# Attention of a hybrid backbone: one loop of iterations over all units, and softmax maps combined by two GpSimd passes without normalising

## The reference, cut to what matters

```
s  = einsum('bqhcd,bkhcd->bhcqk', q, k) * scale          # c = 0, 1: two maps
pr = softmax(s, axis=-1)
w  = pr[:, :, 0] - lam * pr[:, :, 1]
o  = einsum('bhqk,bkhe->bqhe', w, v)
o  = rms_norm(o, subln_g) * (1.0 - lam_init)              # mean of o*o + 1e-6 under the root
```

## Time and profile before

| | |
|---|---|
| time, median of 3 runs | 4578.49 us |
| span of the profiled execution | 4593.8 us |
| busy: PE, DVE, ACT, POOL | 3727.9, 1665.4, 1256.8, 1175.2 us |
| share of the span: PE, DVE, ACT, POOL | 81, 36, 27, 26% |
| attention, in either layer | 375 us of the span |
| busy in the first layer's attention: PE, DVE, ACT, POOL | 255.8, 231.9, 207.6, 140.8 us |

### The profile page before, as it was taken

The page is one execution under the profiler, slowest core; times in us unless marked ns, Lnnn a source line. Parts: engine busy times, 40 slices in busy tenths (PEclk is TensorE's granted clock), DMA queues, the critical chain, the costliest instruction groups (busy, mean ns, idle before and its releaser), DMA issues. The chain is left out here.

```text
span 4593.8 us, 53336 instructions
## 1 busy us (share of the span) xinstructions
PE 3727.9 (81%) x19468; PEld 3375.5 (73%) x19468; DVE 1665.4 (36%) x1950; ACT 1256.8 (27%) x1848; POOL 1175.2 (26%) x542
## 2 busy tenths in 40 slices
PE   3874999787577799999938849997875777999998
PEld 2664988565466699999926649885664567999998
DVE  4234323254666412121242343232546664121212
ACT  2232122122455412121122321221224563121211
POOL 2011121054343222212120121210543342212211
PEclk8877999888787899999968779998887888999999
DMA  2544211234511111110415442122445111111104
GB/s 85 185 132 182 87 64 71 93 128 160 173 36 45 46 54 65 34 68 30 141 54 185 135 180 87 63 78 88 134 157 167 37 44 53 51 62 37 64 32 149
DMA packets 156156, 428.99 MB, mean 93 GB/s; under 512 B 30202, under 2 KB 51966, under 8 KB 154688
## 3 DMA queue, kind: packets, MB, share of 16 engines
q1 hardware_dynamic: 139936, 379.55, 24.8%
q10 hardware_dynamic: 16128, 48.26, 2.9%
HBM read 312.38 MB, written 120.08 MB: 94 GB/s over the span
## 5 line engine op out<-in xcount | busy, mean ns | idle before, releaser
L2061 POOL TENSOR_TENSOR branch_wl<-branch_raw,branch_wh 128x1536 fp32r<-128x1536 f32 (+1 forms) x72 | 267.3, 3713 | 926.5 <-ACT branch_wh L2021 926.5
L127 PE MATMUL ps<-hh,branch_wh 128*128 128x384 f32 x1728 | 398.2, 338 | 41.2 <-POOL branch_wl L2061 24.2
L127 PE MATMUL ps<-hl,branch_wh 128*128 128x384 f32 x1728 | 396.2, 337 | 0.0
L127 PE MATMUL ps<-hh,branch_wl 128*128 128x384 f32 x1728 | 396.1, 337 | 0.0
L127 PEld LDWEIGHTS ps<-hh,branch_wh 128*128 128x128 f32 x1728 | 311.5, 190 | 44.5 <-issue 44.5
L2092 DVE TENSOR_TENSOR branch_gate<-ps,branch_gate 128x1152 f32<-128x1152 f32 x48 | 65.2, 1358 | 751.8 <-PE ps L127 751.8
L127 PEld LDWEIGHTS ps<-hl,branch_wh 128*128 128x128 f32 x1728 | 311.9, 190 | 0.0
L127 PEld LDWEIGHTS ps<-hh,branch_wl 128*128 128x128 f32 x1728 | 311.5, 190 | 0.0
L1292 POOL TENSOR_TENSOR conv_dl<-conv_draw,conv_dh 128x512 fp32r<-128x512 f32 x128 | 180.2, 1415 | 471.4 <-ACT conv_dh L1242 470.6
L1778 POOL TENSOR_TENSOR attn_prob<-attn_prob 128x1280 f32<-128x1280 f32 (+1 forms) x72 | 190.4, 2644 | 241.1 <-ACT attn_prob L1690 241.1
L127 PE MATMUL ps<-hh,mixin_wh 128*128 128x384 f32 x720 | 167.2, 340 | 102.2 <-POOL mixin_wl L943 97.0
(11 more groups left out here) (262 smaller groups left out, 8421.2 us busy)
## 6 DMA issues: line engine op xcount, KB each, us to landing
branch_raw<-in_w_mo SPq DMA_DIRECT2D x48, 768.0 KB, 4.2
H_dram<-fspec_hout ACTq DMA_DIRECT2D x100, 256.0 KB
fspec_araw<-in_w_ada SPq DMA_DIRECT2D x48, 512.0 KB, 4.6
conv_hs<-H_dram SPq DMA_DIRECT2D x32, 768.0 KB, 4.5
w_in_raw<-in_w_in SPq DMA_DIRECT2D x44, 512.0 KB, 3.8
fspec_draw<-in_dft_taps SPq DMA_DIRECT2D x68, 256.0 KB, 3.0
conv_draw<-in_dft_fwd SPq DMA_DIRECT2D x64, 256.0 KB, 2.6
conv_draw<-in_dft_inv SPq DMA_DIRECT2D x64, 256.0 KB, 2.6
```

What stands on the lines that cost most here:

```text
L127: last = pe.matmul(out, w[:, k, :], x[:, k, cols], start=(k == 0 and n == 0), stop=(k == kt - 1 and n == 2))
L2061: pool.tensor_tensor(wl[:, b, 0:size], raw[:, b, 0:size], wh[:, b, 0:size].bitcast(F32), ALU.subtract).then_inc(S["lo"], 1)
```

## The change

Every engine's body of a head becomes `for i in range(NU)`. In iteration i the same four things are in flight everywhere: scores of unit i+1, softmax of unit i, fill 0 of the transposes of unit i-1, fills 1 and 2 of unit i-2, and the group products and norms some iterations later (`units_of`, `group_at`). Where i-1 or i-2 is below zero, the unit belongs to the head before, so the tail of a head runs inside the first iterations of the next, on all engines. Behind the last head come 5 iterations (`DRAIN`) without new units. The body is written out for head 0, as a loop for heads 1 and 2, for head 3 and for the drain.

The combination changes: instead of `prob0/s0 - lam*prob1/s1`, the weights are `prob0 + ratio*prob1` with `ratio = -lam*s0/s1`. The factor s0 is left in the weights, cancels in the norm, and the constant becomes `EPS*s0*s0` per query (`es`). The DVE pass over `prob0` and the ACT pass over `prob1` are gone; POOL multiplies `prob1` and then adds.

Between heads, ACT also rounds the queries (was DVE). Map 0's key remainder moves from POOL to DVE. The prompt unit's weights have their own buffers `wph` and `wpl`, and the prompt values are split one iteration after the others. SP stores the last groups of a head around the next head's loads.

```
 # DVE, per unit
-chain(dve.reciprocal(rinv[:], total[:, u % 2]))
-chain(dve.tensor_tensor(rinv[:, 1:2], rinv[:, 1:2], lam[:, 3:4], ALU.mult))
-dve.sem_inc(S["rp"], 1)
-dve.tensor_scalar(prob0[:, u % 3, 0:n], prob0[:, u % 3, 0:n], rinv[:, 0:1], None, ALU.mult)
+s0, s1 = total[:, u % 3, 0:1], total[:, u % 3, 1:2]
+dve.reciprocal(rinv[:], s1).then_inc(S["rc"], 1)
+dve.scalar_tensor_tensor(out=es[:, u:u + 1], in0=s0, scalar=EPS, in1=s0, op0=ALU.mult, op1=ALU.mult)
+dve.wait_ge(S["rc"], NU * h + u + 1)
+dve.scalar_tensor_tensor(out=ratio[:, u % 3:u % 3 + 1], in0=s0, scalar=lam[:, 3:4], in1=rinv[:],
+                         op0=ALU.mult, op1=ALU.mult).then_inc(S["rp"], 1)
 # ACT, per unit
-nc.scalar.activation(prob1[:, u % 2, 0:n], prob1[:, u % 2, 0:n], ACT.Copy, scale=rinv[:, 1:2])
 # POOL, per unit
+pool.tensor_tensor(gone[:], ratio[:, u % 3:u % 3 + 1], ratio[:, u % 3:u % 3 + 1], ALU.add)
+pool.tensor_scalar(prob1[:, u % 2, 0:n], prob1[:, u % 2, 0:n], ratio[:, u % 3:u % 3 + 1], None, ALU.mult
+                   ).then_inc(S["sc"], 1)
+pool.wait_ge(S["sc"], NU * h + u + 1)
 pool.tensor_tensor(prob0[:, u % 3, 0:n], prob0[:, u % 3, 0:n], prob1[:, u % 2, 0:n], ALU.add)
 # PE, the order of an iteration
+turn(h, two, 1)
+with_v(h, group_at(i, 4, prev, cur), 0)
+done = group_at(i, 5, prev, cur)
+with_v(h, done, 1)
+turn(h, two, 2)
+scores(h, i + 1, 0)                 # at i = 8: scores(h + 1, 0, 0)
+sums(h, done)
+turn(h, one, 0)
+spread(h, done)
+scores(h, i + 1, 1)                 # at i = 8: scores(h + 1, 0, 1)
+if i == NU - 2 and more: turn_keys(h + 1)
 # ACT, the order of an iteration
+high(h, two, 1, prev)
+softmax(h, i, 0, prev)
+high(h, two, 2, prev)
+take(h, group_at(i, 5, prev, cur))
+softmax(h, i, 1, prev)
+high(h, one, 0, prev)
+if i == 2 and cur: split_values(h, prev)
+if i == 3 and cur: split_prompt_values(h, prev)
+if i == NU - 2 and more: split_keys(h + 1, False); split_rest(h + 1, False)
 # POOL, the order of an iteration
+inverse_root(h, group_at(i, 5, prev, cur))
+combine(h, i)
+if i == 2 and cur: lower_values(h)          # waits for both value splits of ACT
+if i == NU - 2 and more: lower_keys(h + 1)  # map 1 only
 # DVE, the order of an iteration
+maximum(h, i, 0)
+low(h, two, 1)
+maximum(h, i, 1)
+low(h, two, 2)
+if i == NU - 1 and more: split_lower(h + 1, False)
+means(h, done)
+ratios(h, i)
+low(h, one, 0)
+scale(h, done)
 # ACT, between heads
+for c in range(2):
+    nc.scalar.copy(kh[:, c, 0:TS], kraw[:, c, 0:TS]).then_inc(S["kh"], 1)
+nc.scalar.copy(qs[:], qraw[:]).then_inc(S["qh"], 1)
 # DVE, between heads (split_lower), ahead of what split_queries had
+dve.tensor_tensor(kl[:, 0, 0:TS], kraw[:, 0, 0:TS], kh[:, 0, 0:TS].bitcast(F32), ALU.subtract)
-dve.tensor_copy(qs[:], qraw[:]).then_inc(S["qh"], 1)
```

More of the change, by code:

```diff
@@ L1459, in group, with weights, units_of, at @@
             return (TS, P) if g == NPV - 1 else (g * G * P, G * P)
[L1461 to L1473, removed]
+        def weights(big, small, u, at, cnt):
+            if u == QT:
+                return small[:, at:at + cnt, :]
+            q = (u % G) * P
+            return big[:, (u // G) % 2, at:at + cnt, q:q + P]
+        def units_of(i, prev, cur):
+            def at(j):
+                if j < 0:
+                    return (-1, j + NU) if prev else None
+                return (0, j) if cur and j < NU else None
+            return at(i), at(i - 1), at(i - 2)
+        def group_at(i, shift, prev, cur):
+            for d, have in ((-1, prev), (0, cur)):
+                for g in range(NPV):
+                    step = 2 * g + shift if g < NPV - 1 else NU + 3
+                    if have and i - d * NU == step:
+                        return d, g
+            return None
         with nc.Block() as block:
@@ L1495, in load_values, with store @@
                     sp.dma_start(vraw[:, KT], vrows[QT, :, hc]).then_inc(S["v"], 16)
[L1497 to L1508, removed]
+                def store(h, d, g):
+                    sp.wait_ge(S["y"], NPV * h + NPV * d + g + 2)
+                    q0, width = group(g)
+                    sp.dma_start(mix[5, h + d][:, q0:q0 + width], y[:, 0:width]).then_inc(S["st"], 16)
@@ L1510, in body @@
                         sp.wait_ge(S["vl"], h + 1)
+                        sp.wait_ge(S["vlp"], h + 1)
                         load(h + 1)
[L1512 to L1515, removed]
-                load(0)
-                heads(sp, body)
+                    if prev:
+                        store(h, -1, NPV - 1)
@@ L1606, in spread @@
                     last.then_inc(S["bc"], 1)
[L1608 to L1622, removed]
-                            turn_keys(h + 1)
[L1624 to L1641, removed]
-                    spread(h, NPV - 2)
-                    with_v(h, NPV - 1, NU - 1)
-                    sums(h, NPV - 1)
-                    spread(h, NPV - 1)
@@ new lines, in body @@
+                def body(h, prev, cur, more):
+                    for i in range(NU if cur else DRAIN):
+                        now, one, two = units_of(i, prev, cur)
+                        turn(h, two, 1)
[3 more added lines that the diff above has]
+                        turn(h, two, 2)
+                        if now is not None and i + 1 < NU:
+                            scores(h, i + 1, 0)
+                        elif now is not None and more:
+                            scores(h + 1, 0, 0)
+                        sums(h, done)
+                        turn(h, one, 0)
+                        spread(h, done)
+                        if now is not None and i + 1 < NU:
+                            scores(h, i + 1, 1)
+                        elif now is not None and more:
+                            scores(h + 1, 0, 1)
+                        if i == NU - 2 and more:
+                            turn_keys(h + 1)
@@ L1865, in means @@
[L1865 to L1874 removed]
+                                      weights(wh, wph, u, at, cnt).bitcast(F32), ALU.subtract).then_inc(S["wl"], 1)
@@ L1914, in _, with body @@
-                round_queries(0)
-                split_queries(0)
-                for c in range(2):
-                    maximum(0, 0, c)
-                scales(0, 0)
-                for c in range(2):
-                    maximum(0, 1, c)
-                with dve.Fori(0, HEADS - 1) as h:
-                    with chain.loop(h, HEADS - 1, per=2 * NU):
-                        body(h, False)
-                body(HEADS - 1, True)
+                def body(h, prev, cur, more):
+                    for i in range(NU if cur else DRAIN):
+                        now, one, two = units_of(i, prev, cur)
+                        if now is not None:
+                            maximum(h, i, 0)
+                        low(h, two, 1)
+                        if now is not None:
+                            maximum(h, i, 1)
+                        low(h, two, 2)
+                        if i == NU - 1 and more:
+                            split_lower(h + 1, False)
+                        done = group_at(i, 5, prev, cur)
+                        means(h, done)
+                        if now is not None:
+                            ratios(h, i)
+                        low(h, one, 0)
+                        scale(h, done)
```

410 lines of the change are left out of this document (212 added, 198 removed).

## The result

The changed kernel took 4537.61 us (median of 4 runs, 4527.23 to 4550.56), the kernel before 4575.27 us beside it: a ratio of 0.9912, interval 0.9889 to 0.9936. Run once more later it gave 0.9910 (0.9891 to 0.9929). The profiled span fell from 4593.8 to 4548.8 us. So the change gains 38 us where 90 were forecast; the time lies in the upper part of the range.

The account below looks back on a forecast made before the run. No engine is full in attention; a chain of waits across engines bounds it, worst between heads. Per layer -12.8 - 28.0 - 1 - 3 = -45 us, -90 in both: 4578.5 - 90 = 4488 us, range 4434 to 4552.

Parts of the forecast that it names:

- The price of POOL's multiply: GpSimd's new pass over map 1 in each large unit: 1.46 us, at most 2.92, mostly hidden before PE needs the weights.
- high end: Upper end of the forecast range: units 7.2 us, boundaries 45, end unchanged, -13 us a layer, 4552 us.
- The loop formula: POOL's time per large unit, from ratio through multiply and add to the next ratio: 4.2 + x us, x the multiply's price.
- the first rival: POOL becomes the bound in attention and the kernel slower, from a multiply of 4.1 us; 4629 us at 5; chance 0.10.
- The unit at 6.7: Large units in a head's steady part: 6.7 us each instead of 7.68; with value splits, -12.8 us a layer.
- The value split: POOL's value remainder pass at iteration 2, holding up `es` and `ratio`: charged 1.7 us per head, 6.8 per layer.
- The boundary: From unit 7 of a head to unit 2 of the next: 38.9 us each, three 116.7 against 144.7, -28.0 a layer.
- Unit 7 to unit 0: First part of the passage between heads, between starts of map 0's maximum: 21.9 us against 27.2 before.
- Units 0 and 1: First two units of the next head, PE at a low clock: 8.5 us each, 17 against 22.1.
- Start and end: Beginning and end of each layer's attention: -1 us at the start, -3 at the end.
- The second layer: Attention there taken as the same 375 us with the same busy times, so the same gain: -45 us.
- The case "both gain more": Units at 6.3 us and boundaries at 33: -20.8 - 35 - 4 - 5 us per layer, 4449 us; chance 0.12.

Follow-up runs that it names:

- short_multiply: Changed kernel, GpSimd multiplying only the first 768 of map 1's 1280 columns, by the ratio broadcast as a second tensor (output differs): 4485.62 us, ratio 0.9774.
- no_port: Changed kernel with `es` and `ratio` computed by tensor_scalar, their columns fetched as scalars of the instruction instead of as tensors: 4553.97 us, ratio 0.9932.

## Why the prediction was right and wrong

**The price of POOL's multiply** is the step that failed. The prediction took "half of 2.92, 1.46, since it reads one tensor instead of two", with 2.92 as its upper end. It costs 3.52, outside both ends: the nearest rows were two-input passes, and a form missing from the trace was bounded by the number of its inputs. In the first layer the steady parts were to gain 12.8 us and lost 7.6; with a pass of 1.47 us (short_multiply) they gain 11.7. The time is in the range by another path than the one the range allowed for: its high end had units of 7.2 us and boundaries of 45, and the runs have 8.1 with the value split and 37.7. The Trainium skill's "GPSIMD Engine Reference", section "Engine selection", has one-input work on GpSimd at roughly line rate; here the one-input form is slower than the add of two tensors (3.52 against 2.92 us), and the measurement decides.

**The loop formula** of the first rival, 4.2 + x, gave the right number at x = 3.52: 7.7 us per unit, and head 1 without its gap of the value split gives (40.78 - 10.17) / 4 = 7.65. GpSimd became the bound, as that rival said, below the price at which it makes the kernel slower (4.1). But one of its terms is right by luck. It has 0.65 us for `es` and `ratio`, held back until POOL is idle. POOL's own queue is 7.0 us per unit, and the other 0.6 is time in which it stands for `ratio`, as ahead of 1323.15 above; there nothing held `es`, and DVE had waited for the exponential of map 1:

```profile
1322.65 0.16 DVE L1847 RECIPROCAL attn_rinv<-attn_total 128x1 f32<-128x1 f32 x1 [1.23 <-ACT attn_prob L1692]
1322.73 0.14 DVE L1848 SCALAR_TENSOR_TENSOR attn_es<-attn_total 128x1 f32<-128x1 f32 x1
```

no_port agrees: without the hold the unit is no shorter. And the formula stops holding as x falls: at 1.47 it gives 5.7, where 6.8 is measured.

**The unit at 6.7** was right for the price assumed, as short_multiply shows (141.9 us for 20 units and the value splits, 140.8 forecast).

**The value split** at 1.7 us a head was too small on a full POOL: 10.17 - 7.65 = 2.5 us. POOL's queue has the two splits, 3.25 us from start to start, between two units. `es` took 2.76 us beside them. The Trainium skill's "SBUF — State Buffer", section "Who interferes with whom", has a VectorE instruction with two SBUF inputs contend with a GpSimd instruction that reads SBUF; the trace agrees. But that is not what makes the gap: in no_port, where nothing holds `es`, it is 10.39.

**The boundary**, 38.9 us forecast, took 37.8, by two errors that cancel. Unit 7 to unit 0 took 23.3 us instead of 21.9; with the short multiply it is 21.7, so this is the same step again. Units 0 and 1 took 14.5 instead of 17 (13.2 with the short multiply), a term that was mis-sized on its own. The prediction took the clock there as low, and the rows have it high: 1.00 in that stretch (1362.50 to 1377.00), which is 2.4 GHz, behind 21.5 us at 0.76 in which PE was busy 13.3 us. The kernel before has 0.65 there:

```profile
1378.80:1401.00 22.20, 16.91 (x77) 14.39 (x76) 9.89 (x17) 8.23 (x14) 4.11 (x3) 0.65 0.04 15
```

How much of the 2.5 us is the clock's was not separated.

**Start and end** together were to fall by 4 us a layer. From the first DVE instruction to the last, less the steady parts and boundaries, they rose from 74.7 to 75.5 in the first layer and from 73.5 to 77.3 in the second. Why is open.

**The second layer** was taken as a copy of the first, "the same 375 us with the same busy times". The busy times are the same, but its attention was 367.2 us long and its boundaries 139.3 instead of 144.7, so there was less to gain.

**SP's store behind the loads** costs nothing in the kernel after, as forecast: no wait of DVE for it is in the trace. It is cover, not absence: with the values split later it costs 5.2 us in each of the two middle heads.

The account against the forecast's changes of -12.8, -28.0 and -4: in the first layer steady parts +7.6, boundaries -31.5, start and end +0.8, together -23.1; in the second +7.4, -24.8 and +3.8, together -13.6. Both make -36.7, beside 37.7 between the medians. Of the 53 us missing from the 90, 40.6 lie in the steady parts. The span of the profiled executions fell by 45.0; the 8.3 beyond attention lie in stages whose code did not change, and one execution each doesn't say more about it.

**The case "both gain more"** has a wrong sum: boundaries of 33 us make 144.7 - 99 = 45.7, not 35, so the time at its own terms would be about 4428 us and not 4449, below the low end of the range. No run came there.

## What to carry to other kernels

A form of instruction that no row shows has no upper bound from a row of another form: before work moves to an engine, that engine's loop should be written as a function of the unknown price, as the rival did, and the forecast be made to depend on it. A queue that is in order hides costs until something ahead of it moves: after each step that shortens the unit, the next wait was a small instruction or a store behind a wait that had been free before. And a pass belongs where it is off the chain from scores to exponentials, even if the engine there takes longer for it (here 2.32 and 2.92 us on GpSimd against 1.54 on VectorE). A second layer with the same busy times is not the same layer: it should be cut by its own rows before its gain is counted.

## What the hardware showed that was not expected

- GpSimd, 128x1280, fp32: tensor times column scalar 3.52 us, times constant 3.45, add of two tensors 2.92, times a column broadcast as second tensor 2.32; 768 columns of the last 1.47.
- A 128x1 VectorE operation with two tensor inputs in SBUF took up to 2.85 us beside a GpSimd pass (0.14 at the shortest); with the same columns given as scalars, `es` took 0.20 and `ratio` 0.27 us, at most 0.28 in both layers.
